# The order of projection and mixing products on TensorE in a hybrid decoder layer

## The reference

```python
proj = rmsnorm(x, g_mix_pre) @ w_in              # split into q, k, v, r, glr, u, vs
g    = log_sigmoid(glr @ w_gla_gate + b) / 16    # 4 heads, keys of 64, values of 128
# per chunk of 64 tokens, b = cumsum(g):
o    = (q * exp(b)) @ S + masked(scores(q, k, b)) @ v
S    = exp(b_last) * S + (k * exp(b_last - b)).T @ v
o    = rmsnorm(o, g_gla_out) * silu(r)
s    = gelu(u) * (tril(W_s) @ layernorm(gelu(vs)) + b_s)   # mix over 128 positions
x    = x + rmsnorm(concat(o, s) @ w_out, g_mix_post)
x    = x + rmsnorm(conv_ffn(rmsnorm(x, g_ffn_pre)), g_ffn_post)
x    = x + rmsnorm((p @ w_ple) * sigmoid(rmsnorm(x, g_ple_in) @ w_ple_gate), g_ple_post)
```

## Time and profile before

| what | value |
|---|---|
| median of three runs | 2732.08 us |
| the profiled execution's own time | 2734.14 us |
| its span, first to last instruction | 2732.4 us |
| mean granted TensorE clock | 0.976 |
| PE matmuls busy | 2617.1 us (96%) |
| PE weight loads busy | 2355.2 us (86%) |
| DVE busy | 1046.5 us (38%) |
| ACT busy | 880.5 us (32%) |
| POOL busy | 501.6 us (18%) |

### The profile page before, as it was taken

How to read it: one execution, slowest core, us unless ns; L and a number is a source line. 1 busy time by engine, 2 the same in 40 slices (tenths; PEclk the granted TensorE clock), 3 DMA queues, 4 the chain that set the end, 5 groups by cost and what they waited for, 6 DMA issues and landing times. The chain is left out here.

```text
span 2732.4 us, 36970 instructions
## 1 busy us (share of the span) xinstructions
PE 2617.1 (96%) x13712; PEld 2355.2 (86%) x13712; DVE 1046.5 (38%) x1706; ACT 880.5 (32%) x1781; POOL 501.6 (18%) x611
## 2 busy tenths in 40 slices
PE   7999999779999899999999999999899999979998
PEld 5779999667777799999999999999688888867887
DVE  4200000177884644444444444444422343314332
ACT  4311111244453433333333333333412232214332
POOL 2100000135554111111111111111000022321222
PEclk9999999878999999999999999999999999998999
DMA  4311222364344311111111111112644576543221
GB/s 149 100 59 61 70 70 70 99 152 133 103 127 148 118 56 37 56 38 55 40 53 40 53 40 53 40 53 76 192 120 113 134 240 195 168 128 111 76 86 43
DMA packets 271138, 256.44 MB, mean 94 GB/s; under 512 B 16936, under 2 KB 233228, under 8 KB 271020
## 3 DMA queue, kind: packets, MB, share of 16 engines
q1 hardware_dynamic: 271058, 255.40, 30.6%
HBM read 178.89 MB, written 76.46 MB: 93 GB/s over the span
## 5 line engine op out<-in xcount | busy, mean ns | idle before, releaser
L2067 PE MATMUL up_acc<-xh,up_wh 128*128 128x416 f32 x1760 | 619.6, 352 | 0.0
L2067 PE MATMUL up_acc<-xl,up_wh 128*128 128x416 f32 x1760 | 616.5, 350 | 0.0
L2067 PE MATMUL up_acc<-xh,up_wl 128*128 128x416 f32 x1760 | 616.1, 350 | 0.0
L1998 DVE SCALAR_TENSOR_TENSOR up_conv<-up_up,ffn_features,up_conv 128x416 f32<-128x416 f32 (+1 forms) x440 | 284.0, 645 | 570.1 <-ACT up_conv L1920 557.9
L2067 PEld LDWEIGHTS up_acc<-xh,up_wl 128*128 128x128 f32 x1760 | 330.1, 188 | 4.2
L2067 PEld LDWEIGHTS up_acc<-xl,up_wh 128*128 128x128 f32 x1760 | 330.8, 188 | 2.8
L2067 PEld LDWEIGHTS up_acc<-xh,up_wh 128*128 128x128 f32 x1760 | 329.9, 187 | 2.9
L1914 ACT ACTIVATE up_up<-up_acc 128x416 f32<-128x416 f32 (+1 forms) x220 | 113.3, 515 | 606.2 <-PE up_acc L2067 606.2
L2399 PE MATMUL down_acc<-down_wh,down_sh 128*128 128x512 f32 x748 | 292.6, 391 | 12.3 <-DVE down_wl L2311 10.3
L2399 PE MATMUL down_acc<-down_wh,down_sl 128*128 128x512 f32 x748 | 292.0, 390 | 0.0
L2399 PE MATMUL down_acc<-down_wl,down_sh 128*128 128x512 f32 x748 | 292.0, 390 | 0.0
(11 more groups left out here) (301 smaller groups left out, 4201.3 us busy)
## 6 DMA issues: line engine op xcount, KB each, us to landing
lanes<-hidden SPq DMA_DIRECT2D x33, 1408.0 KB, 7.5
hidden<-up_conv SPq DMA_DIRECT2D x110, 208.0 KB, 1.9
up_raw<-in_w_up SPq DMA_DIRECT2D x44, 512.0 KB, 3.9
proj_features<-in_outs SPq DMA_DIRECT2D x60, 208.0 KB, 1.9
up_x_area<-in_w_down SPq DMA_DIRECT2D x40, 256.0 KB, 5.4
in_raw<-in_w_in SPq DMA_DIRECT2D x19, 512.0 KB, 4.3
lanes<-x SPq DMA_DIRECT2D x17, 512.0 KB, 4.1
in_x<-in_x_prompt SPq DMA_DIRECT2D x16, 512.0 KB, 3.7
```

The source lines that it names most:

```text
L1998: last = nc.vector.scalar_tensor_tensor(out=out, in0=x(c), in1=out, scalar=taps[:, at, c:c + 1].rearrange("p a c -> p (a c)"), op0=ALU.mul ...
L2067: last = nc.tensor.matmul(acc[b][:, 0:TB], w[kind][:, k, :], x[:, k, b * TB:(b + 1) * TB], start=(k == 0 and p == 0), stop=(k == KC - 1 an ...
```

## The change

In the mixers' loop of PE, the nine first matmuls of the projection of tile t - 2, with their waits, stand ahead of the front of tile t in every step from t = 2 on; before, they did so in step 2 alone. No instruction is added or removed, and the other engines' programs are the same.

```diff
             for t in range(LAST):
-                if t != 2:
+                if t < 2:
                     mix_front(t)
                 if projects(t - 2):
                     project(t - 2, 0, range(0, 3))
-                if t == 2:
+                if t >= 2:
                     mix_front(t)
                 if mixes(t - 1):
                     average_squares(t - 1)
```

## The result

| kernel | median of the runs | lowest to highest | profiled execution |
|---|---|---|---|
| before | 2732.57 us | 2726.98 to 2734.01 | 2734.14 us, span 2732.4 |
| changed | 2774.81 us | 2769.63 to 2783.91 | 2777.84 us, span 2776.1 |

Both medians are of four runs (for the kernel before one more than the three named above). The change makes the kernel slower by a ratio of 1.0162, 95% interval 1.0144 to 1.0180. The forecast was 2778.

A forecast was written before the change was run, and what follows sets the result against it. PE, busy 96% of the span, bounds the kernel, so its order and stands matter. 29.0 + 2.5 + 1.8 = 33.3 us, plus 13 us of clock, makes 46 us on 2732.1: 2778 us, range 2755 to 2808.

The forecast's parts named there:

- The cover lost: PE before the projection, t = 3 to 15: the front no longer hides the 2.8 us release chain; 29.0 us together.
- steps 4 and 8: Steps where PE already waits for scaled rows: DVE comes 0.9 us later in each, together 1.8 us.
- What is late next: DVE's mask starts 3.2 us later, PE only 2.28, so PE waits for the head norm: 2.5 us.
- The small waits: PE before outputs within chunks: 0.1 to 0.2 us in ten steps, 0.7 without sample work; for the states, nothing.
- my slow-clock excuse for step 4: Head norm wait at t = 4: the slow clock gives PE more work time, so the 0.7 us wait was not expected there.
- The clock: PE's clock in the mixers' stage falls to half after some 7 of 12 new stands: 13 us, ends 0 and 41.
- That the clock holds: Rival: new stands in the mixers' stage do not lower PE's clock, only t = 8 might; 2765, up to 2768 us; chance 0.25.
- it falls everywhere: Rival: PE's clock falls in every step for as long as at t = 4; 74 us, 2806 us; chance 0.12.
- nothing was there for the projection to fill: Rival, steps 3 to 15: not slower, the projection fills the front's waits; at best 8 us gained, 2724 us; chance 0.03.
- PE passed no waiting matmul: Rival: PE would take the front past the waiting projection, so nothing changes; 2732 us; chance 0.04.
- the harmless one: A PE stand of 1.99 us in the profile before, after which the clock stayed at 1.00; new stands are a little longer.

The follow-up runs named there:

- The filled kernel: Changed kernel plus eight unused 512-column matmuls ahead of the waiting projection in steps 3 to 15: 2766.79 us, ratio 1.0139 to the kernel before.
- The other kernels of the new order: Changed kernel with gate logits and turned keys back ahead of the projection (2766.12 us), or with the root from the first 512 columns' squares alone (2750.33 us).
- the kernel with three ahead: Changed kernel with only three of the projection's nine matmuls ahead of the front from t = 3, six behind it: 2793.05 us, ratio 1.0231 to the kernel before.

## Why the prediction was right

**The cover lost.** 29.0 us were forecast, and 1.8 us more for steps 4 and 8, 30.8 in all. The waits on `mix_y` grew from 4.9 to 33.9 us, by 29.0. A single stand is 2.11 to 2.3 us, not 2.28 throughout: PE comes to its state products up to 0.1 us later (815.24 - 814.81 = 0.43 us after the last matmul's start, where it was 729.38 - 729.06 = 0.32), as these now wait for DVE's states, and the chain runs meanwhile. Step 6's is 1.80.

**What is late next.** The mask was to start 3.2 us later against PE. From the state products to the mask it was 732.71 - 729.38 = 3.33 us and is 821.81 - 815.24 = 6.57: 3.24. The small waits came to 1.3 us for the norm and 0.4 for the states, where 2.5 was forecast; the wait of some 0.6 us in steps 3 and 4 shows that my slow-clock excuse for step 4 was wrong, and the steps from 8 on wait under 0.1 us.

**The clock.** 13 us were forecast; it cost some 10. From the clocks of the single steps, half-clock time is twice the shortfall times the length: after, for steps 3, 4, 5, 6, 8, 9 and 15, 3.5 + 6.9 + 10.4 + 13.4 + 3.3 + 10.3 + 3.3 = 51 us; before, for steps 4 and 6, 6.6 + 17.2 = 24. Half of the 27 us between, the price that the prediction put on it, is 13.6. The filled kernel shows what it really costs: its half-clock time is back at 24 us (steps 4, 6 and 8), a full step lasts as long as in the changed kernel, and its stage is 297.77 - 287.37 = 10.4 us shorter, 7.8 of them in steps 5 and 9. (PE stands still for a part of the half-clock time, 0.7 of 10.2 us in step 9, and that part costs nothing.) The size was in part luck: I took 7 short stretches in 12 steps; there were five new ones, two of them three times as long, none in steps 10 to 14, and step 6 lost some. The runs' spread of 14 us says so too, and the medians of the two kernels are 8.0 us apart, not 10.4.

**The sum.** 29.0 + 1.7 + 10.4 = 41.1 of the stage's 45.0 us. The rest is in no wait of the list: a step at full clock grew by 20.33 - 17.78 = 2.55 us and its stand is 2.11, since PE is busy for 18.18 us in it and not for 17.78. The other kernels of the new order have these 0.4 us too, whether the stand is 1.10 (18.14) or 0.79 us (18.17). They hold the 0.1 us ahead of the state products and 0.07 us ahead of the outputs within chunks, which start at 827.92, right behind the head norm's end at 827.12 + 0.75 = 827.87; where the rest comes from is not shown. With the half-clock time as before, the stage is 287.37 - 252.73 = 34.6 us longer, and 33.3 was forecast for that.

**The rivals.** That the clock holds would have been 2765, 33 us more than before; the filler brought the half-clock time back to that of before, and 2767 came out, 38 us above the kernel before beside it by the medians and 35 by the stages. That it falls everywhere would have been 2806; the kernel with three ahead is nearly that case, at 2793. The front never waited for its inputs, so nothing was there for the projection to fill; and PE passed no waiting matmul.

**Left open.** Why the clock fell in steps 5 and 9 and not in steps 10 to 14, whose stands are alike, is not shown.

## What to carry to other kernels

Before work is moved ahead on a saturated in-order engine, find what the moved piece waits for and how long that release chain is: here 2.8 us through three engines, which 0.6 us of state products and 2.3 us of front happened to cover exactly, so that an ordinary step showed no wait in the profile before. An engine without gaps can be one edit away from a gap in every round. And a gap on PE can be priced twice, by its length and by the clock behind it; in steps 10 to 14 of the changed kernel it was its length alone.

## What was not expected of the hardware

A stand of 1.10 us, with 1.7 us of small matmuls ahead of it, was followed by half clock in most steps, while 1.99 us elsewhere was not the earlier trace rows; so the length of a stand alone does not decide. Nor do small matmuls ahead of it. The prediction set the new stands, with 0.6 us of these ahead, apart from the harmless one; but that one has 1.91 us of them, which end where it begins:

```profile
1941.70 1.91 PE L2410 MATMUL down_tail_acc<-ident,tail 128*18 128x128 f32 x16
```

What follows may matter as well: after the same 2.2 us, nine matmuls of 512 columns left five steps of thirteen newly slow, three of them followed by the front's small products left every step slow. And no stand is needed at all: step 6 of the kernel before is busy throughout at a mean clock of 0.74, and spacing its small products among matmuls of 512 columns did not help (0.76).
